# Column-group sets of a feed-forward block: both seven-product chunks at the head, partial sums carried between PSUM banks

## What is computed

```python
def _swiglu(h, w_gate_up, w_down):
    gu = h @ w_gate_up
    g, u = gu[..., :D_FF], gu[..., D_FF:]
    return (jax.nn.silu(g) * u) @ w_down

x = x + _swiglu(_rmsnorm(x, norm_ffn[i]), w_gate_up[i], w_down[i])
```

## Time and profile before

| | |
|---|---|
| three runs | 1228.4, 1228.4, 1227.89 us; median 1228.4 us |
| the profiled execution | 1228.27 us, its span from first to last instruction 1226.4 us |
| TensorE (PE) busy | 1219.6 us, 99% |
| VectorE (DVE) busy | 1013.4 us, 83% |
| ScalarE (ACT) busy | 751.4 us, 61% |
| granted TensorE clock | 1.0 |
| chain that ended last | PE 94%, DVE 4%, issue 1%, ACT 1% |

### The profile page before, as it was taken

How to read it: one execution, slowest core, us unless ns; L and a number is a source line. 1 busy time by engine, 2 the same in 40 slices (tenths; PEclk the granted TensorE clock), 3 DMA queues, 4 the chain that set the end, 5 groups by cost and what they waited for, 6 DMA issues and landing times.

```text
span 1226.4 us, 16404 instructions
## 1 busy us (share of the span) xinstructions
PE 1219.6 (99%) x6284; PEld 1013.5 (83%) x6284; DVE 1013.4 (83%) x1436; ACT 751.4 (61%) x1154; POOL 97.9 (8%) x123
## 2 busy tenths in 40 slices
PE   9999999999999999999999999999999999999998
PEld 7778888888888888888888888888888888888887
DVE  8986999889788798878887756988888785989787
ACT  8875756555998655555687536465556643745552
POOL 2520000000100100000232000000001300000000
PEclk9999999999999999999999999999999999999999
DMA  8544455546654564645555234556455315464552
GB/s 342 154 142 138 173 207 187 206 172 206 205 195 169 187 206 172 237 174 206 198 187 172 69 104 145 203 178 230 172 206 190 133 35 206 173 211 166 206 189 86
DMA packets 32830, 218.75 MB, mean 178 GB/s; under 512 B 3936, under 2 KB 4576, under 8 KB 7408
## 3 DMA queue, kind: packets, MB, share of 16 engines
q1 hardware_dynamic: 30384, 210.32, 48.8%
q0 software_dynamic: 1648, 6.88, 2.2%
q10 hardware_dynamic: 720, 0.50, 0.1%
HBM read 216.64 MB, written 1.05 MB: 177 GB/s over the span
## 4 chain that ended last, share of the span: by engine, by line
PE 94%; DVE 4%; issue 1%; ACT 1%; DMA 0%; SPq 0%; DVEq 0%; ACTq 0%
PE PS L521 26%; PE PS L523 26%; PE PS L522 26%; PE PS L527 6%; PE PS L1022 2%; PE PS L1046 1%; PE PS L558 1%; PE PS L630 1%; PE PS L624 1%; PE PS L625 1%; PE PS L556 1%; PE PS L555 1%; DVE WL L2050 1%; DMA RAW<-in_w 0%; PE PS L963 0%
## 5 line engine op out<-in xcount | busy, mean ns | idle before, releaser
L2050 DVE TENSOR_TENSOR WL<-RAW,WH 128x2048 fp32r<-128x2048 f32 (+3 forms) x198 | 420.8, 2131 | 97.8 <-ACT WH L1364 97.8
L1364 ACT ACTIVATE WH<-RAW 128x2048 fp32r<-128x2048 f32 (+3 forms) x200 | 356.6, 1789 | 119.2 <-PE PS L523 119.1
L521 PE MATMUL PS<-WH,HTh 128*128 128x512 f32 (+1 forms) x752 | 296.9, 395 | 0.1
L523 PE MATMUL PS<-WH,HTl 128*128 128x512 f32 (+1 forms) x752 | 291.6, 388 | 0.0
L522 PE MATMUL PS<-WL,HTh 128*128 128x512 f32 (+1 forms) x752 | 291.3, 387 | 0.0
L523 PEld LDWEIGHTS PS<-WH,HTl 128*128 128x128 f32 x752 | 141.2, 188 | 29.4
L521 PEld LDWEIGHTS PS<-WH,HTh 128*128 128x128 f32 x752 | 141.3, 188 | 29.3 <-DVE WL L2050 1.1
L522 PEld LDWEIGHTS PS<-WL,HTh 128*128 128x128 f32 x752 | 141.4, 188 | 26.9
L521 PE MATMUL PS<-WH,YAh 128*128 128x512 f32 x354 | 139.9, 395 | 0.1
L523 PE MATMUL PS<-WH,YAl 128*128 128x512 f32 x354 | 138.0, 390 | 0.0
L522 PE MATMUL PS<-WL,YAh 128*128 128x512 f32 x354 | 137.8, 389 | 0.0
(11 more groups left out here) (546 smaller groups left out, 2051.0 us busy)
## 6 DMA issues: line engine op xcount, KB each, us to landing
RAW<-in_w SPq DMA_DIRECT2D x196, 1024.0 KB, 4.9
WL<-in_w POOLq DMA_DIRECT2D x2, 1024.0 KB, 9.0
BC<-in_rows POOLq DMA_DIRECT2D x4, 512.0 KB, 4.1
YG<-in_mem POOLq DMA_DIRECT2D x4, 512.0 KB, 4.9
X<-in_x SPq DMA_DIRECT2D x2, 512.0 KB, 5.4
RAW<-in_w SPq DMA_DIRECT2D x4, 256.0 KB, 5.7
BC<-in_s SPq DMA_DIRECT2D x1, 512.0 KB, 11.3
YG<-in_s SPq DMA_DIRECT2D x1, 512.0 KB, 9.2
```

Of the source, the lines that this page charges most:

```text
L521: e.matmul(out, ah, bh, start=start, stop=False, skip_group_check=joined)
L523: return e.matmul(out, al, bh, start=False, stop=stop, skip_group_check=joined)
L1364: e.activation(WH[:, c % NW, w], RAW[:, c % NR, w], ACT.Copy).then_inc(S.hi, 1)
L2050: e.tensor_tensor(WL[:, c % NW, w], RAW[:, c % NR, w], WH[:, c % NW, w].bitcast(f32), SUB).then_inc(S.lo, 1)
```

## The change

- The set's two seven-product chunks are now its first and second (c4 and c5, in set 6 c12 and c13), the plain ones its third and fourth. `FAST_AT`, the packing of the chunks and `forms` (slices 0 to 3) follow.
- The seven products of both chunks are added up directly in the four banks of the set's results, in an order that lets a partial sum be finished, read, and used on. ScalarE copies bank C11 into bank C22 (`cu`) and later C22 into C12 (`cv`), and TensorE adds further products onto the copies. One product, M7, is copied to SBUF (`c7`), and VectorE adds it twice from there (`j1`, `j2`). The eight joins of a set are gone; the joins in the second matmul stay.
- The sums of quarters are formed in two turns. Four are formed ahead of the set (`set_raw`, `set_hi`, `set_rest`), four in it, in the places of those that TensorE has read (`late_raw`, `late_hi`). They lie in the first quarter of WH and WL and in YBh and YBl.
- Folds have banks of their own list (`FOLD_BANK`). fold(1) moves from behind the set's first chunk to ahead of its fourth; fold(4) moves from behind group 5 to the same place in set 6, with fold(5); folds 2 and 3 move from behind group 4 into it, 6 and 7 from behind group 8 into it.
- SP loads into a RAW slot of a first chunk after six, of a second after eight of the set's sums.

TensorE, the core of `set_mm` and the callers:

```diff
-BANKS = ((0, 1), (6, 7), (0, 2), (1, 3), (6, 7), (2, 3), (0, 2), (1, 3), (6, 7), (0, 1), (6, 7))
+BANKS = ((0, 1), (6, 7), (4, 2), (5, 3), (6, 7), (0, 1), (4, 2), (5, 3), (6, 7), (0, 1), (6, 7))
+FOLD_BANK = (0, 1, 4, 5, 6, 0, 4, 5, 4, 5, 4)
...
-                plain(cs[0], 0)
-                folds()
-                early_chunk(f, a, True, cs[1])
-                plain(cs[2], 4)
-                early_chunk(f, a, False, cs[3])
+                rests_ready(e, cs[0])
+                bank_free(C11)
+                add(C11, Y(0, 0, 0), W(0, 1), start=True)
+                rests_ready(e, cs[1])
+                add(C11, Y(1, 0, 0), W(1, 1), stop=True).then_inc(S.qa, 1)
+                e.wait_ge(S.gsl, 2 * f + 2)
+                bank_free(C12)
+                add(C12, sum_of(0, 2), T(0, 0, 1), start=True).then_inc(S.qt, 1)
+                add(C12, sum_of(1, 2), T(1, 0, 3), stop=True).then_inc(S.qt, 1)
+                e.wait_ge(S.cu, n + 1)
+                add(C22, sum_of(0, 1), T(0, 1, 2)).then_inc(S.qt, 1)
+                add(C22, sum_of(1, 1), T(1, 1, 4)).then_inc(S.qt, 1)
+                add(C11, Y(0, 1, 0), W(0, 2))
+                add(C11, Y(1, 1, 0), W(1, 2))
+                e.wait_ge(S.j1, n + 1)
+                add(C22, sum_of(0, 0), T(0, 0, 5))
+                add(C22, sum_of(1, 0), T(1, 0, 6)).then_inc(S.qc, 1)
+                rests_ready(e, cs[2])
+                for t, b in enumerate((C11, C21)):
+                    for k in (4, 5):
+                        rows(cs[2], k, t, 0, b)
+                e.wait_ge(S.cv, n + 1)
+                add(C12, sum_of(0, 3), W(0, 3)).then_inc(S.used, 1)
+                add(C12, sum_of(1, 3), W(1, 3)).then_inc(S.used, 1)
+                add(C21, Y(0, 1, 1), T(0, 1, 7))
+                add(C21, Y(1, 1, 1), T(1, 1, 8))
+                e.wait_ge(S.j2, n + 1)
+                for t, b in enumerate((C12, C22)):
+                    for k in (4, 5):
+                        tk = rows(cs[2], k, t, 1, b)
+                tk.then_inc(S.used, 1)
+                folds()
+                rests_ready(e, cs[3])
+                for t in range(2):
+                    for k in (6, 7):
+                        for half in range(2):
+                            tk = rows(cs[3], k, t, half, BANKS[a + half][t])
+                tk.then_inc(S.used, 1)
...
-                group(4)
-                fold(2)
-                fold(3)
+                group(4, lambda: two_folds(2))
                 group(5)
-                fold(4)
-                set_mm(f, 6, cs[12:16], lambda: fold(5))
-                group(8)
-                fold(6)
-                fold(7)
+                set_mm(f, 6, cs[12:16], lambda: two_folds(4))
+                group(8, lambda: two_folds(6))
```

`T(i, j, ready)` waits for that many rests of sums (`tlo`), `bank_free` for the last fold that used the bank. ScalarE (`late_hi` waits for a sum and for `qt`, then rounds it):

```diff
+                def column_set(a, *folds):
+                    feed(cs[2 * a - 1])
+                    e.wait_ge(S.qa, n + 1)
+                    copy(PS[:, C22, :], PS[:, C11, :]).then_inc(S.cu, 1)
+                    e.wait_ge(S.qt, 4 * n + 2)
+                    copy(FB[f][5][:, 3, :], PS[:, C12, :]).then_inc(S.c7, 1)
+                    late_hi(a, 0, 0)
+                    late_hi(a, 1, 0)
+                    tanh(a - 1)
+                    e.wait_ge(S.qc, n + 1)
+                    copy(PS[:, C12, :], PS[:, C22, :]).then_inc(S.cv, 1)
+                    late_hi(a, 0, 1)
+                    late_hi(a, 1, 1)
+                    for g in folds:
+                        fold(g)
+                    feed(cs[2 * a])
...
-                tanh(1)
-                fold(0)
-                sums_hi(cs[5])
-                feed(cs[3])
-                column_set(2)
+                set_hi(2, 1)
+                column_set(2, 0, 1)
...
+                column_set(6, 4, 5)
```

VectorE, the set and its entry in a block:

```diff
+                def column_set(a, *folds):
+                    late_raw(a, 0, 0)
+                    late_raw(a, 0, 1)
+                    late_raw(a, 1, 0)
+                    feed(cs[2 * a - 1])
+                    set_rest(a, 5, 0, 0)
+                    e.wait_ge(S.c7, n + 1)
+                    e.wait_ge(S.qt, 4 * n + 4)
+                    e.tensor_tensor(PS[:, C21, :], PS[:, C22, :], M7, ADD).then_inc(S.j1, 1)
+                    set_rest(a, 6, 1, 0)
+                    late_raw(a, 1, 1)
+                    gate(a - 1)
+                    e.wait_ge(S.cv, n + 1)
+                    e.tensor_tensor(PS[:, C22, :], PS[:, C22, :], M7, ADD).then_inc(S.j2, 1)
+                    set_rest(a, 7, 0, 1)
+                    set_rest(a, 8, 1, 1)
+                    for g in folds:
+                        fold(g)
+                    feed(cs[2 * a])
...
                 gate(0)
                 feed(cs[1])
+                set_raw(2, 0)
                 forms_lo()
+                set_rest(2, 1, 0, 0)
+                set_rest(2, 2, 0, 1)
                 feed(cs[2])
-                sums(cs[5])
-                fold(0)
-                gate(1)
-                sums_lo(cs[5])
-                feed(cs[3])
-                fold(1)
-                column_set(2)
+                set_ahead(2, 1)
+                column_set(2, 0, 1)
```

More of the change, by code:

```diff
@@ L706, in fast_chunk, with set_mm @@
                 mul(2, Y(1, 1), T(3), False).then_inc(S.used, 1)
-            def early_chunk(f, a, first, c):
-                m, i = FASTS[c], 0 if first else 1
+            def set_mm(f, a, cs, folds):
+                n, m0 = set_n(f, a), 4 * FASTS[cs[0]]
+                C11, C21 = BANKS[a]
+                C12, C22 = BANKS[a + 1]
                 GSh, GSl = FB[f][8:10]
[L712 to L753, removed]
-                tk.then_inc(S.used, 1)
@@ L756, in set_mm, with W @@
[L756 to L768, removed]
-                plain(cs[0], 0)
-                folds()
-                early_chunk(f, a, True, cs[1])
-                plain(cs[2], 4)
-                early_chunk(f, a, False, cs[3])
+                def W(i, w):
+                    o, c = slice(512 * w, 512 * w + 512), cs[i]
+                    return WH[:, c % NW, o], WL[:, c % NW, o]
@@ new lines, in Y, with sum_of, add, T @@
+                def Y(i, j, t):
+                    k, ts = 2 * i + j, slice(128 * t, 128 * t + 128)
+                    return HTh[:, k, ts], HTl[:, k, ts]
+                def sum_of(i, q):
+                    w = slice(128 * q, 128 * q + 128)
+                    return GSh[:, i, w], GSl[:, i, w]
+                def add(b, x, w, start=False, stop=False):
+                    return mm3(PS[:, b, :], *x, *w, start, stop, not (start or stop))
+                def T(i, j, ready):
+                    e.wait_ge(S.tlo, m0 + ready)
+                    return set_t(f, a, i, j)
@@ new lines, in rows, with bank_free @@
+                def rows(c, k, t, half, b):
+                    o = (k % 2) * 1024 + half * 512
+                    return product(c, PS[:, b, :], (HTh, HTl), k, t, slice(o, o + 512), False, k == 7, True)
+                def bank_free(b):
+                    for g in in_bank(a, b):
+                        e.wait_ge(S.ylo, fold_n(f, g))
+                rests_ready(e, cs[0])
+                bank_free(C11)
+                add(C11, Y(0, 0, 0), W(0, 1), start=True)
+                rests_ready(e, cs[1])
@@ L2292, in group, with set_raw @@
                     gate(g)
-                def column_set(a):
-                    n, c = SETS.index(a), cs[2 * a + 3]
-                    sums(c)
+                def set_raw(a, i):
+                    c, m0 = cs[2 * a + i], 4 * FASTS[cs[2 * a]]
+                    B12, B11, B21, B22 = (RAW[:, c % NR, 512 * n:512 * n + 512] for n in range(4))
+                    if m0 and i == 0:
+                        e.wait_ge(S.tlo, m0)
+                    e.tensor_tensor(TR_[:, 2 * i, :], B22, B12, SUB).then_inc(S.tr, 1)
+                    e.wait_ge(S.tr, m0 + 2 * i + 1)
+                    e.tensor_tensor(TR_[:, 2 * i + 1, :], TR_[:, 2 * i, :], B11, ADD).then_inc(S.tr, 1)
@@ new lines, in set_rest, with late_raw @@
+                def set_rest(a, n, i, j):
+                    e.wait_ge(S.thi, 4 * FASTS[cs[2 * a]] + n)
+                    hi, lo = set_t(f, a, i, j)
+                    rest(lo, TR_[:, 2 * i + j, :], hi).then_inc(S.tlo, 1)
+                def late_raw(a, i, j):
+                    c, m0 = cs[2 * a + i], 4 * FASTS[cs[2 * a]]
+                    B12, B11, B21, B22 = (RAW[:, c % NR, 512 * n:512 * n + 512] for n in range(4))
+                    e.wait_ge(S.tlo, m0 + 2 * i + j + 1)
+                    if j == 0:
+                        e.tensor_tensor(TR_[:, 2 * i, :], B12, B11, SUB).then_inc(S.tr, 1)
+                    else:
+                        e.tensor_tensor(TR_[:, 2 * i + 1, :], B21, TR_[:, 2 * i + 1, :], SUB).then_inc(S.tr, 1)
```

207 lines of the change are left out of this document (102 added, 105 removed).

## The result

The changed kernel takes **1311.3 us** (median of 4 runs, 1310.41 to 1312.02), against 1228.3 us (4 runs) for the kernel before: ratio 1.0676, 95% interval 1.0658 to 1.0695. That is 83.0 us slower; the prediction had 1308, and rival B began at 1312. The profiled execution took 1310.4 us, its span 1308.6.

The account below looks back on a forecast made before the run. TensorE, 99% busy without slack, was taken to bound the kernel. Stops 49.0, entry 18.6, restarts 1.4, less folds 0.4, gave 68.6 us, 80.0 with the clock: 1228.3 + 80.0 = 1308 us, range 1290 to 1322.

Parts of the forecast that it names:

- rival B: Clock falls in all eight stops, or comes back later: 1312 us, up to 1327 with twice the price; chance 0.23.
- The stops behind the folds: TensorE waits for the fourth chunk's split behind the folds: 4.96 us in set 2, 7.3 in set 6, together 49.0.
- The entry: Ninth product waits for VectorE's join: set 2 late 4.2 or 3.1 us, set 6 late 1.0; together 18.6 us.
- restarts: Slow first matmuls after waits on TensorE: two in each of eight sets at 0.09 us, adding 1.4 us.
- products that wait for ScalarE's copies in PSUM: Sign of a wrong prediction: TensorE waiting for ScalarE's PS copies, read as the price of bank to bank.
- just hidden: In set 6, ScalarE's copy into C22 ends at 2.7 us and is wanted at 2.72, behind four products.
- The copy from bank to bank: ScalarE's PSUM copy, without an earlier row, taken at 0.60 us; bounds 0.3 and 1.2 us.
- Folds, -0.4 us: Nine groups of transposes in a block become eight: four breaks of TensorE's matmuls saved at 0.09 us, 0.4 us gained.
- The clock, 11.4 us: TensorE's clock falls in the four long stops and two of the four short ones: 6 x 1.9 us.
- A: The clock holds through the stops, which stay as forecast: 1297 us; chance 0.20.
- C: Only one wait is real: 1248 us if the fold stops are covered, 1278 to 1290 if the entry is; chance 0.07.
- D: Not slower: feeds reach one chunk further, with four slots instead of three, or the new order isn't run; 1228 us; chance 0.05.

Follow-up runs that it names:

- run with only the entry left: Changed kernel with the feeds of the set's fourth chunk and the next group's first chunk ahead of the folds, on ScalarE and VectorE: 1248.3 us.
- run with the shorter stops: Changed kernel with the feed of the set's fourth chunk ahead of the folds on ScalarE alone: 1310.9 us.
- best order tried: Two-feeds-ahead kernel plus two plain TensorE rows of c6 ahead of the wait for j1, and ScalarE's c6 split before rounding the second sums: 1240.2 us.

## Why the prediction was right

**The stops behind the folds, 49.0 us: right.** They measure 4.97 and 7.32 us in the first block, 49.2 over the eight. The run with two feeds ahead removes them wholly, so their cause is the place of the feed in two queues. The steps of the chain came out within 0.01 us each, because every one was read from rows of the same instructions: spacings of two in a row, the durations of the split (1.92 us) and the rest (2.29 us), and handovers of 0.03 us. One was a stand-in: VectorE's 0.28 us for ScalarE's short copy, which took 0.28.

**The entry, 18.6 us and 1.4 for restarts: right.** In the first block 4.3 us (4.2 predicted), in the third 3.15 (3.1). The run with only the entry left is 19.9 us over before. What the sum did not separate is which wait it is: I took VectorE's queue for the one chain, and the waits for cu and tlo as lying inside it. In set 2 the copy's wait of 1.3 us is the longest of the four, since it stands behind c6's split. The sum survived this, since the ninth product waits for j1 in either case. The prediction had named products that wait for ScalarE's copies in PSUM as a sign that it was wrong, for the price of such a copy. The list has them, 5.1 us in four waits, but the copy's price isn't the reason: its place in the queue is. With VectorE's adds cut to an eighth, 5.6 us remained. The larger part is in set 2, mostly by ScalarE's queue. The rest is some 0.3 us in each set 6, where in the first block of that run the copy into C22 starts at 194.75 behind the split of c14, ends at 195.33 and is followed by the product at 195.38; the prediction had this copy just hidden.

**The copy from bank to bank: right**, 0.58 us for 0.60. **Folds, -0.4 us:** no run takes this term by itself.

**The clock, 11.4 us: the term that was mis-sized.** The step "in the four long stops and in two of the four short ones" failed: it fell in all eight, 2.0 to 4.9 us behind the last matmul instead of about 4. The 1.9 us for each, taken from the program's start, was a little high: 12.9 us by the run with idle matmuls is 1.6 each, with 8.5 slow matmuls on average where the start had nine. That the two errors partly cancel is luck. That is rival B's condition (all eight) at a price below B's, and the time came out between the forecast and B.
The Trainium skill, TensorE: Matmul & The Clock Gate, section "HAM oscillation — how this bites in real kernels", has the clock fall in the wait between two bursts, so that each burst starts slow. Seven of the eight stops agree; in the eighth the clock fell 0.1 us behind the start. The section doesn't have the case of the run with the shorter stops, where in the first stop the burst started at full rate and the clock fell 1.4 us into it.

**The sum.** 49.2 + 19.9 + 12.9 = 82.0 of the 83.0 us measured; the folds' gain is inside the 19.9, which is a difference to the kernel before. The 1.0 us over is not attributed; the run with only the entry left has its own small share of the clock in it.

**Rivals.** A (the clock holds, 1297) is what the run with idle matmuls gives, 1298.4. C (only one wait real, 1248 where the stops are covered) is what the run with both feeds ahead gives, 1248.3: the case exists, but in another kernel. D needed a fourth slot; the split of c7 starts 1.13 us behind the transposes, as its place in the queue says.

**What could be mended.** The best order tried, 1240.2 us, is still 1.0% slower than before. The change takes no matmul away, and TensorE had no wait in the blocks before, so nothing beyond the four saved breaks was there to win.

## What to carry to other kernels

Where TensorE has no slack, write down for every chunk what stands ahead of its split in each engine's queue, and what of that waits for TensorE itself: a split behind the copy of a transpose that TensorE makes just before that chunk is a serial chain, and one place earlier in the queue was worth 54 us here. An edit that shortens a stop may bring nothing while the stop is still long enough for the clock to fall: hold the clock with idle matmuls once, and the two parts can be read apart.

## What was not expected of the hardware

- When the clock fell was no fixed time after the last matmul: 3.9 us in the stop of the first set 6, 4.6 in that of the first set 2, and from 2.0 us (set 2 of the second block, last transpose to 476.82, fall at 478.86) to 4.9 us (set 2 of the fourth) over the eight. With ScalarE's feed ahead the fall in the first set 2 came after TensorE had already run again at full rate for 1.4 us, so that 3.6 us of idleness cost more than 4.8 us: 10 matmuls at half rate against 8.
- It also fell in entries with no wait over 1.3 us, where TensorE was busy for 4.48 of 7.09 us. There it isn't the same in every execution of a kernel: the four runs with one feed ahead have mean clocks of 0.997, 0.997, 1.000 and 0.999 at 1257.1, 1257.2, 1255.8 and 1257.9 us. What decides it stays open, and the last of these shows that it isn't all of the spread.
- A first matmul behind a wait has its successor 0.33 to 0.34 us later (171.84 to 172.18), not 0.227, at the full rate: 0.1 us for every wait seen here, beside the idle time that the list of waits shows. That idle time is itself 0.16 us short of the delay, since it counts from the end of a record of 0.39 us.
